# A conditioned decoder layer: x loaded first, six ring buffers for modulation weights, grouped bias rows, small loads on the sync queue, modulation products later

## What is computed

```python
c_act = silu(c)
sh_a, sc_a, gt_a, sh_f, sc_f, gt_f = split(c_act @ ada_w + ada_b, 6)   # 6 x 1024 columns
h = rmsnorm(x, norm_mix_g) * (1 + sc_a) + sh_a
g_q, g_k, g_v, g_g, g_a, s_q, s_k, s_v = split(h @ w_in)
o_gla = gla_mixer(g_q, g_k, g_v, g_g, g_a, ...)     # gated linear attention, 4 heads
o_swa = swa_sink_mixer(s_q, s_k, s_v, sinks, cos, sin)   # window 128, 8 query heads
x = x + gt_a * (concat(o_gla, o_swa) @ w_out)
h = rmsnorm(x, norm_ffn_g) * (1 + sc_f) + sh_f
x = x + gt_f * hier_moe(h, ...)                     # top 2 of 8 experts in one of 4 groups
return rmsnorm(x, final_norm_g)
```

## Time and profile before

| | |
|---|---|
| median of 3 runs | 588.59 us (588.34 to 588.6) |
| profiled execution, span | 591.2 us |
| TensorE busy | 512.2 us, 87% |
| VectorE busy | 284.6 us, 48% |
| ScalarE busy | 147.1 us, 25% |
| mean granted TensorE clock | 0.938 |
| moved by DMA | 163.88 MB, mean 277 GB/s |

### The profile page before, as it was taken

How to read it: one execution, slowest core, us unless ns; L and a number is a source line. 1 busy time by engine, 2 the same in 40 slices (tenths; PEclk the granted TensorE clock), 3 DMA queues, 4 the chain that set the end, 5 groups by cost and what they waited for, 6 DMA issues and landing times.

```text
span 591.2 us, 7201 instructions
## 1 busy us (share of the span) xinstructions
PE 512.2 (87%) x2644; PEld 292.3 (49%) x2644; DVE 284.6 (48%) x700; ACT 147.1 (25%) x370; POOL 80.2 (14%) x128
## 2 busy tenths in 40 slices
PE   0497999999999998999983999999888987797981
PEld 0353585545656565455653555555444544344430
DVE  4589817484747473555554256323112321123275
ACT  2502214142434270222030312222111321120221
POOL 5000000000100000001122222222122221111101
PEclk9989889979999999999995899999889998798996
DMA  8999962950970005691017999999999999999673
GB/s 292 377 346 277 343 250 81 386 178 0 267 302 2 1 1 213 257 369 60 25 71 253 357 395 398 414 414 407 399 414 417 387 415 418 391 388 420 257 303 142
DMA packets 57981, 163.88 MB, mean 277 GB/s; under 512 B 10339, under 2 KB 13940, under 8 KB 51034
## 3 DMA queue, kind: packets, MB, share of 16 engines
q1 hardware_dynamic: 46632, 147.95, 66.0%
q0 software_dynamic: 6192, 12.38, 5.6%
q10 hardware_dynamic: 5122, 3.08, 1.8%
HBM read 155.48 MB, written 16.58 MB: 291 GB/s over the span
## 4 chain that ended last, share of the span: by engine, by line
PE 63%; DMA 14%; SPq 13%; DVE 3%; issue 3%; ACT 1%; ACTq 1%; POOL 1%; POOLq 0%; DVEq 0%
PE ps L1572 22%; PE ps L1840 10%; PE ps L1751 9%; DMA early<-in_w_up 6%; SPq L498 5%; PE ps L1853 4%; SPq L502 3%; DMA wide<-in_w_up 2%; SPq L504 2%; DMA xres<-in_x 2%; DMA wide<-y_rows 2%; PE ps L1829 2%; ACTq L772 1%; PE ps L1777 1%; PE ps L1617 1%
## 5 line engine op out<-in xcount | busy, mean ns | idle before, releaser
L1572 PE MATMUL ps<-ring,hreg 128*128 128x512 f32 (+1 forms) x320 | 136.6, 584 | 2.1 <-DVE hreg L1053 2.1
L1572 PEld LDWEIGHTS ps<-ring,hreg 128*128 128x128 f32 x320 | 63.5, 203 | 65.5 <-issue 60.0
L1440 DVE TENSOR_TENSOR turned<-turned,ps 64x256 f32<-64x256 f32 x33 | 14.0, 423 | 135.5 <-ACT turned L949 135.5
L1840 PE MATMUL ps<-ring,proj 128*64 128x256 f32 x288 | 70.6, 401 | 7.8 <-DMA ring<-in_w_up 7.2
L1841 PE MATMUL ps<-ring,proj 128*64 128x256 f32 x288 | 70.6, 401 | 0.0
L1840 PEld LDWEIGHTS ps<-ring,proj 128*64 128x64 f32 x288 | 40.2, 144 | 31.0 <-DMA ring<-in_w_up 7.6
L1024 DVE SCALAR_TENSOR_TENSOR wide<-wide,csil 128x512 f32<-128x512 f32 x72 | 49.1, 746 | 2.5 <-DMA wide<-in_ada_w 2.5
L949 ACT ACTIVATE turned<-ps 64x256 f32<-64x256 f32 x33 | 12.4, 375 | 143.7 <-PE ps L1841 143.7
L701 POOL DMA_INDIRECT y_rows<-proj,hreg x31 | 30.9, 997 | 109.8 <-DVE proj L1446 109.8
L643 POOL TENSOR_TENSOR rstd<-ssq,halfm 128x1 f32<-128x1 f32 (+1 forms) x13 | 10.0, 766 | 232.6 <-DVE ssq L1323 140.5
L1841 PEld LDWEIGHTS ps<-ring,proj 128*64 128x64 f32 x288 | 40.3, 145 | 0.0
(11 more groups left out here) (331 smaller groups left out, 792.7 us busy)
## 6 DMA issues: line engine op xcount, KB each, us to landing
wide<-in_ada_w SPq DMA_DIRECT2D x24, 1024.0 KB, 8.7
ring<-in_w_gate SPq DMA_DIRECT2D x17, 1024.0 KB
ring<-in_w_up SPq DMA_DIRECT2D x17, 1024.0 KB
ring<-in_w_down SPq DMA_DIRECT2D x17, 1024.0 KB, 23.5
wide<-in_w_down SPq DMA_DIRECT2D x10, 1024.0 KB
ring<-in_w_in SPq DMA_DIRECT2D x4, 2048.0 KB, 9.6
proj<-in_w_gate SPq DMA_DIRECT2D x5, 1024.0 KB
proj<-in_w_up SPq DMA_DIRECT2D x5, 1024.0 KB
```

The source lines that it names most:

```text
L1572: mm = pe.matmul(ps[bank_of(st)][:, 0:CW[ch]], hT[:, k, b * P:(b + 1) * P], win_sb[ch][:, k, :], start=k == 0, stop=k == KD - 1)
L1840: pe.matmul(ps[bank][0:TILE, 0:F], hx[k], w_cols(w, 0, k), start=k == 0, stop=k == KD - 1)
```

## The change

SyncE loads x first, then the bias rows and pieces. The first six halves of the modulation weights (pieces 0, 2, 1) go to the memory of `w_in` chunks 4, 3 and 2 in `ring`, which are loaded later and now wait until the halves are used up; halves 6 on use the three buffers in `wide` as before. The 12 bias rows come as three groups of four rows on partitions 0, 32, 64 and 96. The nine small loads are issued by SyncE behind chunk 1 of `w_in`. On VectorE the mean of squares is made ahead of piece 0; on TensorE the columns of x are turned block by block ahead of `sum_columns(0)`. In the list, mod 4 moves behind proj 0,3, mod 5 behind proj 1,1, mod 7 and amp behind proj 2,0, mod 9 behind proj 2,3, and mod 10 to mod 11, behind proj 3,1. Existing semaphores are used a second time, which changes their counts in a few waits.

```diff
 MIXER_ORDER = (
-    [("ada_sum", 4), ("ada_sum", 5), ("proj", 0, 0), ("proj", 0, 1), ("mod", 4), ("ada_sum", 6), ("proj", 0, 2),
-     ("proj", 0, 3), ("mod", 5), ("ada_sum", 7), ("proj", 1, 0), ("low_turn",), ("proj", 1, 1),
-     ("proj", 1, 2), ("mod", 7), ("proj", 1, 3), ("rope",), ("decay_logit",), ("amp",), ("log_sigmoid",)] +
-    [("proj", 2, 0), ("ada_sum", 8), ("proj", 2, 1), ("decay",), ("attn_turn", 0), ("ada_sum", 9),
-     ("proj", 2, 2), ("mod", 9), ("attn_score", 0), ("attn_exp", 0), ("ada_sum", 10), ("ada_sum", 11),
-     ("proj", 2, 3), ("mod", 10)] +
-    _projected(0, ("proj", 3, 0), ("proj", 3, 1), [("mod", 11)]) + _projected(1, ("proj", 3, 2), ("proj", 3, 3)) +
+    [("ada_sum", 4), ("ada_sum", 5), ("proj", 0, 0), ("proj", 0, 1), ("proj", 0, 2), ("proj", 0, 3), ("mod", 4),
+     ("ada_sum", 6), ("proj", 1, 0), ("low_turn",), ("proj", 1, 1), ("mod", 5), ("ada_sum", 7), ("proj", 1, 2),
+     ("proj", 1, 3), ("rope",), ("decay_logit",), ("log_sigmoid",)] +
+    [("proj", 2, 0), ("mod", 7), ("amp",), ("decay",), ("ada_sum", 8), ("proj", 2, 1), ("attn_turn", 0),
+     ("ada_sum", 9), ("proj", 2, 2), ("attn_score", 0), ("attn_exp", 0), ("proj", 2, 3), ("mod", 9),
+     ("ada_sum", 10), ("ada_sum", 11)] +
+    _projected(0, ("proj", 3, 0), ("proj", 3, 1), [("mod", 10), ("mod", 11)]) + _projected(1, ("proj", 3, 2), ("proj", 3, 3)) +
...
+        early_sb = [ring[:, at_c[ch] + i * KH * PC:at_c[ch] + (i + 1) * KH * PC].rearrange("p (k n) -> p k n", k=KH)
+                    for ch in (4, 3, 2) for i in range(2)]
+        EARLY = len(early_sb)
+        def ada_half(q):
+            return early_sb[q] if q < EARLY else ada_sb[(q - EARLY) % 3]
...
+            def biases(g):
+                if g:
+                    sp.wait_ge(bias_added, 4 * g)
+                parts = ada_b.rearrange("l (a i n) -> (l a) i n", a=len(PARTS), i=2)
+                for a in range(2):
+                    sp.dma_start(brows[2 * a:2 * a + 2, :], parts[PARTS[2 * g + a]]).then_inc(brow_in, 16)
...
             def win(ch):
                 lo, hi = CHUNKS[ch]
+                if ch >= 2:
+                    sp.wait_ge(ada_rows, KH * 2 * (5 - ch))
...
-            piece(0)
             for b in range(NB):
                 sp.dma_start(xres[:, b, :], x_v[b]).then_inc(x_in[b], 16)
+            biases(0)
+            piece(0)
             piece(2)
             win(0)
             piece(1)
             piece(3)
             win(1)
-            for i in range(4, 8):
-                piece(i)
...
+            piece(4)
+            biases(1)
+            piece(5)
             win(2)
+            piece(6)
+            piece(7)
+            win(3)
             piece(8)
+            biases(2)
             piece(9)
-            win(3)
+            win(4)
             piece(10)
-            win(4)
             piece(11)
...
-            piece(0)
             dve.wait_ge(ssq_ready, NB)
             dve.tensor_scalar(ssq[:, 0:NB], ssq[:, 0:NB], 1.0 / D, EPS, ALU.mult, ALU.add).then_inc(mean1_ready, 1)
+            piece(0)
...
+            for b in range(NB):
+                pe.wait_ge(xs_ready, b + 1)
+                for k in range(4):
+                    mm = pe.transpose(ps[X_BANK[k]][:, b * P:(b + 1) * P], scm[:, b, k * P:(k + 1) * P], ident[:, :])
+                    if b == NB - 1:
+                        mm.then_inc(x_turned, 1)
             sum_columns(0)
-            pe.wait_ge(xs_ready, NB)
-            for k in range(4):
-                turn_x(k)
             sum_columns(2)
```

More of the change, by code:

```diff
@@ L160, in layer_kernel @@
         o_ = 3 * KH * PC
+        early_sb = [ring[:, at_c[ch] + i * KH * PC:at_c[ch] + (i + 1) * KH * PC].rearrange("p (k n) -> p k n", k=KH)
[3 more added lines that the diff above has]
+            return early_sb[q] if q < EARLY else ada_sb[(q - EARLY) % 3]
         acc = wide[:, o_:o_ + 2 * PC].rearrange("p (a n) -> p a n", a=2)
         acc2 = wide[:, o_ + 2 * PC:o_ + 3 * PC]
-        brow = wide[0:1, o_ + 3 * PC:o_ + 4 * PC]
+        brows = wide[0:P:32, o_ + 3 * PC:o_ + 4 * PC]
+        brow = [wide[32 * i:32 * i + 1, o_ + 3 * PC:o_ + 4 * PC] for i in range(4)]
         wout_sb = wide[:, :].rearrange("p (k n) -> p k n", k=KD)
@@ L421, in layer_kernel, with half_landed @@
         y_in = [[y_in0, y_in1, y_in2, y_in3], x_in]
+        ada_in = [ada_in0, ada_in1, ada_in2]
+        early_in = [h_st0, h_st1, h_st2, h_st3, fg_in, out_done]
+        def half_landed(q):
+            return (early_in[q], 16) if q < EARLY else (ada_in[(q - EARLY) % 3], 16 * ((q - EARLY) // 3 + 1))
         block = ctx.enter_context(nc.Block())
@@ L457, in piece, with few @@
                     q = 2 * n + kh
-                    if q >= 3:
+                    if q >= EARLY + 3:
                         sp.wait_ge(ada_rows, KH * (q - 2))
[L460 to L464, removed]
+                    sp.dma_start(ada_half(q), ada_v[:, kh * KH:(kh + 1) * KH, col:col + PC])\
+                        .then_inc(half_landed(q)[0], 16)
+            def biases(g):
[4 more added lines that the diff above has]
+                    sp.dma_start(brows[2 * a:2 * a + 2, :], parts[PARTS[2 * g + a]]).then_inc(brow_in, 16)
+            def few(o, i):
+                sp.dma_start(o, i).then_inc(small_in, 16)
             def win(ch):
                 lo, hi = CHUNKS[ch]
+                if ch >= 2:
+                    sp.wait_ge(ada_rows, KH * 2 * (5 - ch))
                 sp.dma_start(win_sb[ch], w_in_v[:, :, lo:hi])\
                     .then_inc([win_in0, win_in1, win_in2, win_in3, win_in4][ch], 16)
-            piece(0)
             for b in range(NB):
                 sp.dma_start(xres[:, b, :], x_v[b]).then_inc(x_in[b], 16)
+            biases(0)
+            piece(0)
             piece(2)
@@ L478, in _ @@
             win(1)
-            for i in range(4, 8):
-                piece(i)
+            with nc.allow_non_contiguous_dma("broadcast loads of small vectors"):
+                few(sinks[:, :], swa_sinks[0:1, :].broadcast_to([P, SH]))
+                few(gla_g[:, :], gla_norm_g.rearrange("l h v -> l (h v)").broadcast_to([P, GH * DV]))
+                few(wa2[0:RANK, :], gla_w_a2[0])
+                few(wa2[RANK:RANK + 1, :], gla_b_a2)
+                few(fcol[:, 2, :], norm_ffn_g.rearrange("l (p k) -> p (l k)", k=KD))
+                few(wr[:, :, 0:NG], w_grp.rearrange("l (p k) n -> p (l k) n", k=KD))
+                few(wr[:, :, NG:], w_exp.rearrange("l (p k) n -> p (l k) n", k=KD))
+                few(br[:, 0:NG], b_grp[0:1, :].broadcast_to([P, NG]))
+                few(br[:, NG:], b_exp[0:1, :].broadcast_to([P, NE]))
+            piece(4)
+            biases(1)
+            piece(5)
             win(2)
+            piece(6)
+            piece(7)
+            win(3)
             piece(8)
+            biases(2)
             piece(9)
-            win(3)
+            win(4)
             piece(10)
-            win(4)
             piece(11)
@@ L531, in _ @@
             for b in range(NB):
-                sp.wait_ge(h_stored[b], 16)
+                sp.wait_ge(h_stored[b], 2 * 16)
             gates(4, 4)
@@ L585, in _ @@
                     sp.dma_start(out_v[b][:, cols], xres[:, b, cols]).then_inc(out_done, 16)
-            sp.wait_ge(out_done, 16 * 2 * NB)
+            sp.wait_ge(out_done, 16 * (2 * NB + 1))
         @block.gpsimd
@@ L682, in _ @@
             for b in range(NB):
-                pool.wait_ge(h_stored[b], 16)
+                pool.wait_ge(h_stored[b], 2 * 16)
             pool.wait_ge(hg_init, 4)
@@ L789, in _ @@
                                bias=mcol[:, 1, k:k + 1]).then_inc(h_act, 1)
[L791 to L800, removed]
             act.wait_ge(ang_ready, 1)
@@ L1014, in piece @@
                     if k % KH == 0:
-                        dve.wait_ge(ada_sem[q % 3], 16 * (q // 3 + 1))
-                    w = ada_sb[q % 3][:, k % KH, :]
+                        dve.wait_ge(*half_landed(q))
+                    w = ada_half(q)[:, k % KH, :]
                     to = a if k % 2 == 0 else acc2
@@ L1025, in piece @@
                                                  op0=ALU.mult, op1=ALU.add).then_inc(ada_rows, 1)
-                dve.wait_ge(brow_in, 16 * (n + 1))
+                dve.wait_ge(brow_in, 32 * (i // 4 + 1))
                 dve.wait_ge(ada_rows, KD * n + KD - 1)
-                dve.tensor_tensor(a[0:1, :], a[0:1, :], brow, ALU.add).then_inc(bias_added, 1)
+                row = slice(32 * (i % 4), 32 * (i % 4) + 1)
+                dve.tensor_tensor(a[row, :], a[row, :], brow[i % 4], ALU.add).then_inc(bias_added, 1)
                 dve.wait_ge(ada_rows, KD * (n + 1))
@@ L1532, in finish @@
                 if b == 0:
-                    dve.wait_ge(fg_in, 16)
+                    dve.wait_ge(fg_in, 2 * 16)
                 for i in range(2):
```

6 lines of the change are left out of this document (1 added, 5 removed).

## The result

The changed kernel is slower, not faster: 593.18 us (median of 5, 589.73 to 594.41) against 588.59 us for the kernel before (median of 5 in the same comparison), a ratio of 1.0097 with a 95% interval of 1.005 to 1.0143. The forecast was 587.4 in a range of 585.0 to 589.8. A repetition with 12 executions beside 35 of the kernel before gave 591.66 against 588.14, ratio 1.008 (1.0046 to 1.0114). Executions more than 1.5% above the fastest of their kernel are left out of every ratio here; the 30 of the 35 that are left have a median of 586.89, so the loss is 4.8 us by the medians and 4.7 by the ratio.

The account below looks back on a forecast made before the run. TensorE was taken to bound the kernel up to 230 us. At block 0's probabilities -2.9, surcharge +1.7 and mod 10 +0.86 gave -0.3, or -2.0; the middle, -1.2, from 588.6 gave 587.4 us, range 585.0 to 589.8.

Parts of the forecast that it names:

- What bounds the kernel: Up to 230 us TensorE bounds: whatever it is spared moves everything behind it, unless another engine becomes the later one.
- One for one: Expert stage behind the mixer: moves as a block with the mixer's end, neither more nor less.
- The opening: Start to first projections: x first makes VectorE finish piece 2's column sums later, +0.5 us, bounds -0.5 to +1.5.
- The queue is full from the first microsecond: Loads at the start: DMA queue full throughout, so removing SyncE's waits is worth nothing.
- The small loads: Before mod 4: moving nine loads from ScalarE to SyncE removes 3.71 us idle and 1.96 of half clock, -5.7 us.
- The new wait: At block 0's probabilities: mod 9 behind proj 2,3 delays VectorE's scaling; TensorE idles 3.3 to 5.0 us, then +1.7 surcharge.
- the fall behind mod 7: Projection steps after mod 7: low clock costs 3.4 us, or 1.7 if it lasts half as long.
- late pieces would be covered by the later mods: At mod 4 and 5: pieces 4 and 5, delayed about 2 us, have seven microseconds of cover, so cost nothing.
- I apply the difference to the median: Final step: difference reckoned from the 591.2 us profiled execution, applied to the 588.59 median: 588.6 - 1.2 = 587.4.
- The sum -0.3 to -2.0: Total change up to block 0's probabilities and just behind: -0.3 us, or -2.0 with the shorter clock fall behind mod 7.
- Of the rivals the third: After the idle at block 0's probabilities: clock low twice as long, opening slips; +1.4 (590.0 us) to +2.4; 15%.
- no gain is left: Threshold at block 0's probabilities: the gain vanishes when the idle's clock surcharge passes 3.2 us.

Follow-up runs that it names:

- the two combinations: Kernel before with moved small loads and new list, mod 9 back: ratio 0.9952; changed kernel with mod 9 back and w_in's third chunk behind pieces 6, 7: 0.9975.

## Why the prediction was wrong

**What bounds the kernel.** Right in the main: between the traces the span follows the mixer's end to within 3.4 us. Span less begin of the output projection lies between 351.4 and 354.8 us in all thirteen traces. "One for one" holds no closer than that, and 3.4 us is more than the gain that was forecast. The trace of before had the longest of these tails; that is the 3 us by which its span differed from the changed kernel's at the same mixer end.

**The opening.** Right in sign, wrong in mechanism and too small. VectorE's later order, the only ground given for +0.5, moved the column sums by 0.14 us in the first trace; the rest of the 1.0 was the low clock behind the early turning of x, which the prediction did not have. In the second trace the projections began at 31.59, 2.1 us late and outside the stated bound of +1.5. The last two projections of the opening, at 48.48 in the earlier trace rows, began at 49.82 and 50.66. "The queue is full from the first microsecond" is not so either: in the trace of before the DMA share is 0.39 from 0 to 4 us and above 1 from 4 to 32 us.

**The small loads.** The idle of 3.71 us went. The other part of the term, 1.96 us called half clock, was one execution's: behind the same idle (3.79 us) the second trace of before has 0.26 at mod 4, at a granted clock of 1.00, and nothing on the projections. In time the small loads alone were worth 1.6 to 2.4 us, not 5.7. And the term was credited to the wrong edit: with the new list the idle goes without the loads.

**The new wait.** Right in mechanism: VectorE's pieces 10 and 11 behind mod 9 hold up the scaling, the wait was 3.3 to 5.0 forecast, 3.8 and 5.1 measured, the surcharge on the projection behind it 1.7 forecast, 1.7 measured in the first trace and 0.4 in the second, where the transposes ahead of it took 0.7 more. TensorE at the probabilities at 135.8, with 136.0 forecast, is in part luck: mod 4 came 1.0 us later than reckoned (63.7, not 62.7) and the fall behind mod 7 cost 1.5 us on the projection, not 3.4. In the second trace, where mod 4 came at 64.6 and the projection behind mod 7 took 9.92 us, it was 138.1. In the trace of before the fall behind mod 7 cost 3.0 us (6.75 against the 3.77 of the second trace of before), not the 3.4 of the sum. Right too that late pieces would be covered by the later mods.

**The step that failed is "I apply the difference to the median".** The sum -0.3 to -2.0 was a difference to an execution whose clock had fallen fully behind the idle, behind mod 7 and behind mod 9. Those surcharges (1.96, 3.4 and the one behind mod 9) were treated as costs of the kernel before. They are not: in two other executions of it the first two are absent and the third is smaller, and block 0's probabilities are reached at 133.1 and 133.4 instead of 138.9. Put into the prediction's own sum, the new kernel's 136.0 stands against 133.1, +2.9 instead of -2.9; with 1.7 and 0.86 behind it +5.5, and the output projection did begin 5.7 to 6.3 us later (236.6 and 237.0 against 230.9 and 230.7). The loss of time, 4.7 us by the ratio, is less than these 6, because the part behind the mixer was shorter in the changed kernel: 351.4 and 352.4 us against 353.2 and 354.2. Why it is shorter was not tried.

**What the clock can still do in the changed kernel.** The chain runs through VectorE from mod 9 to the probabilities: 14.95 us in both traces, whatever TensorE's clock does. An execution in which the clock falls for a shorter time behind mod 9 gains nothing from it, it only waits longer. The slices behind mod 9 show it, first in the trace with the wait of 3.8 us, then in the one with 5.1 us:

```profile
120.00:124.00 4.00, 4.00 (x8) 2.12 (x8) 3.19 (x6) 0.18 (x1) 0.00 (x0) 0.50 0.02 4
124.00:128.00 4.00, 4.00 (x7) 1.58 (x6) 3.86 (x8) 0.00 (x0) 0.00 (x0) 0.67 0.77 262
```

```profile
120.00:124.00 4.00, 4.00 (x16) 3.47 (x16) 0.82 (x3) 0.39 (x2) 0.00 (x0) 0.97 0.01 4
124.00:128.00 4.00, 4.00 (x7) 1.73 (x6) 4.00 (x7) 0.00 (x0) 0.00 (x0) 0.60 0.36 91
```

That is 6.6 us at the lower level and 3.4 us. Behind the wait the clock fell in both. It is tempting to say that the new wait took away just the good executions and so made the spread smaller, from 10 us to 4. The wait alone does not explain it: with mod 9 back, where the wait is 0.2 us, the spread is 4.4 us over 12 executions, and in the two combinations 4.4 and 4.7, while the runs with the list of before have 5.7 to 8.6 over the executions that count. So the small spread goes with the new list, with the wait or without it, and why is open. Of the rivals the third had the right side but the wrong cause: the clock behind the new idle was low for one short stretch, not for two. The surcharge from which on "no gain is left" is 2.0 us by the prediction's own sum (-2.9 + 0.86), not 3.2.

The rule of the Trainium skill (DMA: Bandwidth & Descriptors, "Issuing engines are not separate DMA queues"), that the choice of the issuing engine only saves sequencer time, usually little: on the kernel before that time was 8 us in front of an engine that TensorE waited for, and moving it took away a wait of 3.7 us in the trace and gave 1.6 us by the ratio, with an interval that touches no change. In the new list the wait was gone before the loads were moved, so there they had none to remove.

Open: why the clock falls behind the same weak stretch in one execution and not in the next, why the executions of the new list differ less, and what x first costs in time, apart from its trace, is not settled.

## What to carry to other kernels

Before a difference is reckoned from one trace, see whether that execution is the median one: compare its granted clock and span with those of the timed runs, and write every half-clock surcharge as "in this execution". When a producer step is moved later on the bounding engine, follow who waits for it on the next engine and what stands behind it there; here one 3.6 us stage in a later place put 15 us of VectorE's work between two steps of TensorE, and moving it back gave 5.4 to 5.8 us in the traces, more than the wait of 3.8 and 5.1 us: a slow stretch behind the wait went with it.

## What the runs showed of the hardware

Behind the same idle of 3.4 to 3.8 us of TensorE, in the kernel before, the granted clock fell in one execution (0.57 from 60 to 64) and did not in two others. The column sums of mod 7, eight one-column products of 3.6 us, were followed by 0.50 and 0.65 in one execution of the kernel before and by 1.00 in two. Behind the waits at block 0's probabilities the clock fell in the four traces with 1.8, 3.6, 3.8 and 5.1 us and not in the two with 0.2 and 1.0. For a kernel of 588 us the executions on one chip spread over 10 us (8.7 over those that count), and the time has a correlation of -0.81 to the mean granted clock.
